# A fused encoder step: another order for the final norms, and larger last weight transfers

## The reference

```python
# per token: group by argmax, top 2 of the group's 8 experts, their weights in gate
hb = jax.nn.silu(xb @ w_gate[e]) * (xb @ w_up[e])     # (rows, 1024) @ (1024, 512)
y  = (hb @ w_down[e]) * gate                          # (rows, 512) @ (512, 1024)
x  = x + sum over the token's two experts of y
y_prompt, y_sample = rms_norm(x, final_norm_g)        # 512 rows, 64 rows
```

## Time and profile before

| | us |
|---|---|
| median of 3 runs | 1126.94 |
| lowest and highest run | 1126.05, 1127.9 |
| the profiled execution, its own time | 1129.78 |
| its span, from first to last instruction | 1128.04 |

### The profile page before, as it was taken

One profiled execution on the slowest core, in us unless ns is written; L12 is line 12 of the kernel. 1 busy time (PEld: TensorE's weight loads), 2 busy tenths in 40 slices (PEclk: granted clock), 3 DMA queues, 4 the chain that ended last, 5 costly groups with the idle time before them and its releaser, 6 DMA issues.

```text
span 1128.0 us, 11900 instructions
## 1 busy us (share of the span) xinstructions
PE 1045.7 (93%) x4726; PEld 542.4 (48%) x4726; DVE 461.2 (41%) x782; ACT 188.0 (17%) x489; POOL 98.9 (9%) x152
## 2 busy tenths in 40 slices
PE   8999999999999999999999999998886899977895
PEld 4577744555555447776656433333332233333331
DVE  4158734663773033013226753333322233322326
ACT  0156133434133001122101010000000000000001
POOL 1200001112005000000000010010000000000002
PEclk9999999999999999999999999998998899999998
DMA  7621140232234343221085899999999999999996
GB/s 262 242 71 35 46 154 1 69 124 85 76 112 154 135 149 149 75 84 67 1 338 196 352 373 426 428 427 426 426 427 426 428 426 426 427 426 426 421 412 241
DMA packets 52312, 281.14 MB, mean 249 GB/s; under 512 B 8200, under 2 KB 10160, under 8 KB 38946
## 3 DMA queue, kind: packets, MB, share of 16 engines
q1 hardware_dynamic: 45474, 262.57, 58.0%
q0 software_dynamic: 4752, 8.86, 2.1%
q10 hardware_dynamic: 2032, 8.96, 1.9%
HBM read 272.30 MB, written 22.81 MB: 262 GB/s over the span
## 4 chain that ended last, share of the span: by engine, by line
PE 78%; DMA 11%; SPq 5%; DVE 3%; issue 2%; ACT 0%; DVEq 0%; POOL 0%; ACTq 0%; POOLq 0%
PE banks L530 25%; PE banks L953 15%; PE banks L512 14%; DMA arena<-in_exp_w_down_dram 8%; PE banks L941 7%; SPq L1213 4%; PE banks L534 3%; DMA arena<-expert_rows 2%; PE banks L797 2%; PE score_pair L771 2%; DMA arena<-in_w_in_dram 1%; PE score_pair L596 1%; PE score_pair L900 1%; PE banks L630 1%; PE banks L499 1%
## 5 line engine op out<-in xcount | busy, mean ns | idle before, releaser
L530 PE MATMUL banks<-arena 128*128 128x512 f32 x640 | 283.9, 597 | 3.1 <-DMA arena<-in_w_in_dram 1.3
L953 PE MATMUL banks<-arena 128*64 128x512 f32 x1024 | 238.7, 623 | 34.8 <-issue 32.9
L530 PEld LDWEIGHTS banks<-arena 128*128 128x128 f32 x640 | 118.4, 190 | 144.4 <-issue 138.5
L953 PEld LDWEIGHTS banks<-arena 128*64 128x64 f32 x1024 | 82.1, 143 | 186.9 <-issue 185.6
L512 PE MATMUL banks<-arena 128*128 128x288 f32 x640 | 156.1, 406 | 0.0
L512 PEld LDWEIGHTS banks<-arena 128*128 128x128 f32 x640 | 121.4, 190 | 33.8 <-issue 0.4
L941 PE MATMUL banks<-arena 128*64 128x512 f32 x480 | 109.8, 611 | 19.2 <-DMA arena<-in_exp_w_down_dram 12.2
L1426 ACT ACTIVATE arena<-banks 128x512 f32<-128x512 f32 (+6 forms) x135 | 61.7, 493 | 388.9 <-PE banks L530 126.2
L1649 ACT ACTIVATE arena<-banks,arena 128x512 f32<-128x512 f32 x17 | 11.7, 687 | 405.8 <-PE banks L953 381.8
L941 PEld LDWEIGHTS banks<-arena 128*64 128x64 f32 x480 | 36.4, 140 | 82.2 <-issue 68.9
L2218 DVE SCALAR_TENSOR_TENSOR arena<-banks,arena 128x512 f32<-128x512 f32 x34 | 25.4, 750 | 99.6 <-PE banks L941 92.0
(11 more groups left out here) (333 smaller groups left out, 964.3 us busy)
## 6 DMA issues: line engine op xcount, KB each, us to landing
arena<-in_exp_w_gate_dram SPq DMA_DIRECT2D x28, 2048.0 KB, 32.9
arena<-in_exp_w_down_dram SPq DMA_DIRECT2D x28, 2048.0 KB, 33.5
arena<-in_exp_w_up_dram SPq DMA_DIRECT2D x27, 2048.0 KB, 35.2
arena<-in_w_in_dram SPq DMA_DIRECT2D x6, 2048.0 KB, 8.2
arena<-in_exp_w_down_dram SPq DMA_DIRECT2D x16, 512.0 KB, 11.0
arena<-in_exp_w_up_dram SPq DMA_DIRECT2D x6, 1024.0 KB, 8.2
expert_rows<-arena SPq DMA_DIRECT2D x4, 1152.0 KB, 7.8
out_dram<-arena SPq DMA_DIRECT2D x4, 1024.0 KB, 10.4
```

Source lines behind the costliest of these rows:

```text
L530: ins = mm(b[:, :], x, w[:, k, :], start=k == 0, stop=k == KC - 1)
L953: ins = mm(bank[own, :], xgT[:, k, own], w[j][:, k, :], start=k == 0, stop=k == KC - 1)
```

## The change

It has six parts, all in the last two passes and in what follows them.

1. Pass 15's gate matrices come as one transfer of 2 MB each, and its up matrices as two of 1 MB each. Down stays in four. PE waits once for the gate pieces, before its first step, and twice for up.
2. In pass 14, between gate and up, PE runs three matmuls into bank 5 whose result nobody reads.
3. The sample's two reads of `expert_rows` are issued first, then tiles 0, 1, 2, and tile 3 in two transfers, first all first rows and then all second rows (512 KB each).
4. On PE, after placing tiles 0, 1, 2, the sample follows at once, and tile 3 comes last.
5. DVE sums a tile's two read rows before it needs the placed rows (tiles 0 and 1). POOL does that sum for tile 2. For tile 3 DVE adds the placed rows to the first rows, then finishes tile 2, then adds the second rows. The order of the norms is 0, 1, sample, 2, 3.
6. ACT scales the sum of squares and adds epsilon (a second, one-column activation), and POOL only raises to the power.

```diff
-        late_ld = [[sem(f"last_{name}_quarter_loaded{k}") for k in range(4)] for name in ("gate", "up", "down")]
+        late_ld = [[sem(f"last_{name}_piece_loaded{k}") for k in range(n)] for name, n in (("gate", 1), ("up", 2), ("down", 4))]
...
-        FINAL_ORDER = (0, 1, 2, SAMPLE, 3)
+        FINAL_ORDER = (0, 1, SAMPLE, 2, 3)
...
-            def from_rows_by_quarters(bank, w, landed, signal):
+            def from_rows_by_pieces(bank, w, landed, signal):
...
-                    if k % 2 == 0:
-                        pe.wait_ge(landed[k // 2], 32)
+                    if k % (KC // len(landed)) == 0:
+                        pe.wait_ge(landed[k * len(landed) // KC], 32)
...
                     from_rows(SP_, i, banks[0], w[0:2], SP_.g_full, (1, 3, 5) if i == 0 else ())
+                    if i == PAIRS - 2:
+                        for _ in range(3):
+                            mm(banks[5], ident, ident.unsqueeze(1).broadcast_to([P, 4, P]), start=True, stop=True)
...
-            for t in range(SAMPLE):
-                if t == 3:
-                    pe.wait_ge(part_added, 1)
+            for t in range(3):
...
             ins.then_inc(f_full, 1)
+            pe.wait_ge(fsum, 1)
+            for half in range(2):
+                ins = place_last(3, half, True, True)
+            ins.then_inc(f_full, 1)
...
-            def load_quarters(which, e, over):
+            def load_pieces(which, e, over):
...
-                kq = 1 if which == 2 else 2
-                for k in range(4):
+                pieces = len(late_ld[which])
+                kq = (4 if which == 2 else KC) // pieces
+                for k in range(pieces):
...
+            t0, rows = TILES[SAMPLE]
+            for k in range(2):
+                sp.dma_start(yg_both[DEC * k:DEC * (k + 1), :], y_pairs[t0:t0 + rows, k, :]).then_inc(yg_ld[SAMPLE], 16)
+            for t in range(3):
+                t0, rows = TILES[t]
+                sp.dma_start(yg_rows[t], y_pairs[t0:t0 + rows].rearrange("t k n -> t (k n)")).then_inc(yg_ld[t], 16)
+            t0, rows = TILES[3]
+            sp.dma_start(yg[3][0], y_pairs[t0:t0 + rows, 0, :]).then_inc(yg_ld[3], 16)
+            sp.dma_start(yg[3][1], y_pairs[t0:t0 + rows, 1, :]).then_inc(last_row_ld, 16)
...
+            po.wait_ge(yg_ld[2], 16)
+            g.tensor_tensor(yg[2][0], yg[2][0], yg[2][1], ALU.add).then_inc(count_ready, 1)
             for done, t in enumerate(FINAL_ORDER):
                 rows = TILES[t][1]
                 po.wait_ge(fssq, done + 1)
-                inv_std(rstd[0:rows, 17 + t:18 + t], ssq[0:rows, 17 + t:18 + t], D).then_inc(frstd, 1)
+                g.tensor_tensor(rstd[0:rows, 17 + t:18 + t], ssq[0:rows, 17 + t:18 + t], neghalf[0:rows, :], ALU.pow).then_inc(frstd, 1)
...
+                act.wait_ge(sq_done, done + 1)
+                f(total_sq, total_sq, ACT.Copy, bias=EPS, scale=1.0 / D).then_inc(fssq, 1)
...
-            for t in range(3):
-                add_rows(t)
+            sum_rows(0, 1)
+            add_placed(0)
+            sum_rows(1, 2)
+            add_placed(1)
             ve.wait_ge(gf_ready, 1)
             finish(0)
-            add_rows(3)
-            for t in (1, 2, SAMPLE, 3):
-                finish(t)
+            finish(1)
+            ve.wait_ge(count_ready, 2)
+            add_placed(2)
+            finish(SAMPLE)
+            ve.wait_ge(yg_ld[3], 16)
+            ve.wait_ge(f_full, 5)
+            tt(halves(yg[3][0]), halves(yg[3][0]), placed[3], ALU.add).then_inc(part_added, 1)
+            finish(2)
+            ve.wait_ge(part_added, 3)
+            ve.wait_ge(last_row_ld, 16)
+            tt(yg[3][0], yg[3][0], yg[3][1], ALU.add).then_inc(fsum, 1)
+            finish(3)
```

More of the change, by code:

```diff
@@ L425, in encoder @@
         over_done = sem("over_passes_done")
-        y_zero, count_ready, hot_last_ready = sem("y_rows_zeroed"), sem("token_count_ready"), sem("last_one_hot_ready")
-        f_full, part_added = sem("last_rows_placed"), sem("first_row_added")
+        y_zero, count_ready, hot_last_ready = sem("y_rows_zeroed"), sem("token_count_then_row_sum_ready"), sem("last_one_hot_ready")
+        f_full, part_added = sem("last_rows_placed"), sem("two_rows_summed")
         gf_ld, gf_full, gf_ready = sem("final_gain_loaded"), sem("final_gain_spread"), sem("final_gain_copied")
@@ L430, in encoder @@
         yg_ld = [sem(f"y_rows_loaded{t}") for t in range(NT)]
-        fsum, fssq, frstd, fin_ready = (sem(f"final_{n}") for n in ("sum", "ssq", "rstd", "ready"))
+        last_row_ld = sem("second_y_rows_of_last_tile_loaded")
+        fsum, sq_done, fssq, frstd, fin_ready = (sem(f"final_{n}") for n in ("sum", "squares_summed", "ssq", "rstd", "ready"))
         fin_st = sem("final_stored")
         placed = [all_banks[:, 0:2, :], all_banks[:, 3:5, :], all_banks[:, 2:6:3, :], all_banks[:, 0:2, :], pair[0:DEC, :, :]]
-        FINAL_ORDER = (0, 1, 2, SAMPLE, 3)
+        FINAL_ORDER = (0, 1, SAMPLE, 2, 3)
         A = PsumRing(banks[0:3], a_full, a_free)
@@ L1004, in _ @@
                 if i == PAIRS - 1:
-                    from_rows_by_quarters(banks[0], w[0:2], late_ld[0], SP_.g_full)
+                    from_rows_by_pieces(banks[0], w[0:2], late_ld[0], SP_.g_full)
                     pe.wait_ge(gf_ld, 16)
@@ L1009, in _ @@
                     ins.then_inc(gf_full, 1)
-                    from_rows_by_quarters(banks[1], w[2:4], late_ld[1], SP_.u_full)
+                    from_rows_by_pieces(banks[1], w[2:4], late_ld[1], SP_.u_full)
                 else:
@@ L1247, in _ @@
                             sp.dma_start(gfin[0:1, :], a["final_norm_g"].rearrange("(o n) -> o n", o=1)).then_inc(gf_ld, 16)
-                        load_quarters(which, e, over)
+                        load_pieces(which, e, over)
             sp.wait_ge(y_st[0], 16 * (PAIRS // 2))
@@ L1683, in _ @@
                     over_loop(act, over_pair)
-            for t in FINAL_ORDER:
+            for done, t in enumerate(FINAL_ORDER):
                 rows = TILES[t][1]
@@ L1690, in _ @@
                 else:
-                    act.wait_ge(f_full, NT)
+                    act.wait_ge(f_full, 4)
                     total = placed[t]
-                f(scratch.rearrange("p (h n) -> p h n", h=2), total, ACT.Square, accum_out=ssq[0:rows, 17 + t:18 + t]).then_inc(fssq, 1)
+                total_sq = ssq[0:rows, 17 + t:18 + t]
+                f(scratch.rearrange("p (h n) -> p h n", h=2), total, ACT.Square, accum_out=total_sq).then_inc(sq_done, 1)
+                act.wait_ge(sq_done, done + 1)
+                f(total_sq, total_sq, ACT.Copy, bias=EPS, scale=1.0 / D).then_inc(fssq, 1)
         @block.vector
@@ L2296, in halves, with sum_rows, add_placed @@
                 return x.rearrange("p (h n) -> p h n", h=2)
-            def add_rows(t):
+            def sum_rows(t, n):
                 ve.wait_ge(yg_ld[t], 16)
+                tt(yg[t][0], yg[t][0], yg[t][1], ALU.add).then_inc(part_added, 1)
+                ve.wait_ge(part_added, n)
+            def add_placed(t):
                 ve.wait_ge(f_full, t + 1)
-                tt(halves(yg[t][0]), halves(yg[t][0]), placed[t], ALU.add).then_inc(part_added, 1)
-                ve.wait_ge(part_added, t + 1)
-                tt(yg[t][0], yg[t][0], yg[t][1], ALU.add).then_inc(fsum, 1)
+                tt(halves(yg[t][0]), halves(yg[t][0]), placed[t], ALU.add).then_inc(fsum, 1)
             def finish(t):
```

## The result

The changed kernel took 1132.51 us (median of 6 runs, 1131.42 to 1133.37); the kernel before, in runs beside it, 1127.89 (6 runs, 1126.05 to 1129.56). The ratio is 1.0042, interval 1.0030 to 1.0053: 4.6 us slower. I had said 2.45 slower, 1129.4, in 1127.3 to 1131.4. The direction is right, the size is not, and the time lies outside the range. Of the 3.1 us between 1129.4 and 1132.51, 0.95 is the base: I had added to 1126.94, and the kernel before took 1127.89 in these runs. The profiled execution, one of the six, took 1133.37 us. One run in this document, e5's of 1151.05 us, was in the kernel's slower state and is left out of its ratio.

A forecast was written before the change was run, and what follows sets the result against it. It took the weight stream to set the pace, then DVE and the sample's strand. Later tile 2 rows, POOL's sum and tile 3's bare norm moved the end from 1127.55 to 1130.0: 1126.94 + 2.45 = 1129.4, range 1127.3 to 1131.4.

The forecast's parts named there:

- the sample's mixing: Sample's reads ahead of the tiles: slowing of neighbouring transfers beyond their own 1.3 us, bounds 0 and 2.4, taken 1.5 us.
- the tail after tile 2: From the landing of tile 2's rows to the end of the last store: 18.0 us.
- the signs that I had named for a wrong forecast: POOL's sum starting by 1110 or taking 1.3 us, gate starting before 1079, or PE's clock half in gate.
- The wait of part 1: Pass 15's gate on PE waits for both whole matrices: starts 2.75 us later, DVE empties down 2.05 us late.
- the clock rival: PE's clock falls to half before pass 15's gate, costing 1.7 us on PE: 3.2 or 4 us slower; chance 0.30.
- POOL's sum: POOL's add of tile 2's two rows, ahead of its norm steps: 2.35 us, leaving DVE idle 2.7 before finish 0.
- Tile 3's bare norm: At the end, tile 3's norm with no other work to cover it: 2.15 us before its finish.
- Three matmuls: zero: The unread matmuls between gate and up of pass 14 take 2.6 us, absorbed by an idle gap and slack: zero.
- Part 6: nothing: Moving one short norm step from POOL to ACT: worth nothing, bounded by 0.5 us either way.
- The last store: Tile 3's store, now alone at the end: 2.7 us instead of 3.4 behind the sample's slow one.
- The rival that the mixing costs little: The sample's early reads slow neighbours by only 0 to 0.8 us: end 1.0 to 1.7 slower; chance 0.24.
- The faster one: The weight stream gains more than the rates say, 5 us, with 1.4 off the end: 1125.5 us; chance 0.08.

The follow-up runs named there:

- e5: Kernel before with only the sample's read made one 128-partition transfer, still last in the queue, and its sum matrix to match: 1126.21 us, ratio 0.9992.
- e1: Changed kernel with the sample's two 64-partition reads made one 128-partition transfer, and its sum matrix to match: 1131.82 us, ratio 1.0035.
- e4: Changed kernel with pass 15's last gate matrix in four pieces again: 1133.48 us, ratio 1.0055 of the kernel before.
- e8: Changed kernel with the sample's read as one 128-partition transfer and gate in four pieces, POOL's sum of tile 2 kept: 1128.36 us, ratio 1.0011.
- e6: Changed kernel with the sample's read as one 128-partition transfer and DVE summing tile 2, gate in one piece: 1131.87 us, ratio 1.0045 (4 runs).
- e12: The same kernel as e6, run again with more rounds: 1131.14 us, ratio 1.0031 (9 runs).
- e7: As e6 (one 128-partition sample read, DVE sums tile 2), but gate in four pieces again: 1126.87 us, ratio 1.0001.
- e3: Changed kernel with DVE, not POOL, summing tile 2's two read rows, between finishes 0 and 1: 1131.89 us, ratio 1.0036.
- e15: Kernel before with part 1 alone, gate in one transfer for each matrix and up in two: 1128.85 us, ratio 1.0013.
- e11: e9 without the three matmuls in pass 14: 1128.33 us, ratio 1.0006.
- e14: Kernel before with only the three matmuls in pass 14 added: 1127.83 us, ratio 1.0000.
- e9: e7 with DVE's order changed so that the finishes of the sample and tile 2 run during tile 3's norm: 1126.16 us, ratio 0.9990.
- e2: Kernel before with only the sample's two reads issued ahead of the four tiles: 1129.93 us, ratio 1.0020.

## Why the prediction was wrong

**The failed step is a size in part 3: the sample's mixing, "bounds 0 and 2.4, taken 1.5".** The mixing is what the sample's two half-partition transfers cost those in flight beside them, beyond their own length. It measured 4.9 us: 34.51 - 30.70 = 3.8 on down's last weights, and 44.31 - 34.51 = 9.8 from there to tile 2, of which 1.3 + 7.45 are lengths, another 1.05. e1 takes exactly this away (44.31 to 39.42), and e4 against e8 shows 5.0 us of time where nothing else hides it. The whole of the profile's miss of 2.7 us is here: 4.9 - 1.5 = 3.4, less 0.6 because the tail after tile 2 took 17.4 and not 18.0.

The bound was wrong because I read it from before's landings of tiles 2 and 3. There the sample's transfers were the last in the queue, and only the ends of the two tiles still in flight could suffer. Right behind down's weights they slowed all that was in flight with them: 2.39 MB moved in the 10 us at 239 GB/s, which at e1's 414 would have taken 5.8, 4.2 us less, with the DMA engines full in both. The cause is the half-partition form, 64 each, and not short rows or the stride: tile 3's two transfers of 128 partitions have the same 4 KB rows, 8 KB apart, and their packets, 87 of those in the stretch at 413 GB/s of after (1106 to 1110), took 0.16 us each. Reading `expert_rows` beside the weights is not the cause either: e1's single transfer does that, with the same bytes, at 414.

The rule that I weighed, the Trainium skill, page "SBUF — State Buffer", section "Door 1: The DMA port swizzle", has half of the ports out of reach of partitions 0 to 63. The trace agrees with the direction (the 128-partition form cures it), but its price for the sample's own bytes, 1.3 us by my estimate, is a quarter of what was lost in all. None of the signs that I had named for a wrong forecast came up; none of them was about this term.

**A second size was hidden behind it: the strand from the late gate.** The sum without the mixing gives 2.45 - 1.5 = 0.95 us slower. e1 measures that case: ratio 1.0035, 3.9 us, a time (1131.82) above my range by itself. So the right mixing alone would not have saved the forecast. The wait of part 1 was sized rightly: gate started at 1079.21, right on its landing, after 2.59 idle; the landings of gate, 9.79 against 9.80, and of down without the mixing, 30.7, are the forecast's; and in e6, with a full clock, down was emptied at 36.28 against 36.25. In after it does not count, since down waits for weights in any case (e4 gained nothing). It counts once the mixing is gone: 3.4 us from e12 to e7, where 2.05 was priced.

**The rest of that is, in part, the clock rival (0.30).** Behind the unfilled gap the granted clock was half in gate in four profiled executions (e1, e3, e12, e15) and full in two (after, e6). It cost 1.7 us each time. In those four, pass 14's gate had been at half clock too, and in the two it had not: an association in six executions, not a cause. Down fell as well, 1.7 more, in e1, e3 and e12, which I had not priced. But it also fell with gate on time (e8, e11, e14), so it can't all be put down to the late gate. In after's profile the clock did not fall, and if it had, POOL's sum would have covered it. In e3, with both falls, down was emptied at 39.69 and DVE's four adds were done by 44.64, and in after finish 0 starts at 47.37. e3, which has no sum on POOL, ended 0.8 us earlier than after. So the clock isn't the cause of the profile's miss.

**POOL's sum** was sized rightly, 2.35 us, with DVE idle 3.02 before finish 0 (forecast 2.7). With the mixing and the late gate gone it is worth about 1 us by the ratios and 1.5 by the medians (e8 less e7), with overlapping intervals. **Tile 3's bare norm** was 2.14 against 2.15; e9 covers it, and ends 1.4 us ahead of e7 in the profile. **Three matmuls: zero** holds (e14, 1.000). **Part 6: nothing** was not run alone; in after's profile the added one-column activation took 0.20. **The last store**, 2.7 forecast, took 2.6.

The rival that the mixing costs little (0.24) is refuted by e2 and by e4 against e8. The faster one (0.08) is too: the larger pieces brought gate 0.45 and down 0.7 forward, as the rates of the earlier trace rows said, and alone they lengthened the time if anything (e15). The prediction does not show how its 1.4 us came about: its rule of 18.0 us from tile 2's landing gives 2.5 for 5 us less of stream.

The loss of 4.6 us is thus of two strands of nearly the same length in the timed runs. One is the stream with the mixing; the other is PE from the late gate on, with its clock, and POOL's sum where the tiles meet it. Undoing one of them leaves the ratio at 1.0031 to 1.0055 (e1, e3, e4, e12), and only both removed bring it back (e8, 1.0011; e7, 1.0001).

**What stays open.** Why the clock fell behind 2.59 us of idle time in e15 and not behind 2.59 in e6, and how often it does so in pass 15 of the timed runs: they have only the mean granted clock of the whole execution. In e7 the three runs with the lowest mean (0.973 to 0.976) took 1130.1 to 1131.8 us and the other nine 1125.9 to 1128.9; in e12's nine runs time and mean clock show no relation. So how much of the 3.4 us of e12 against e7 is clock was not measured. The part that is only the wait was 1.2 in the profiles (down emptied at 36.28 in e6, 35.08 in e7).

## What to carry to other kernels

A cost read from a transfer's landing holds for the place where the transfer stood. Once it moves in the queue, it must be priced by what is in flight around it, so look at GB/s against the DMA share, and not at its own bytes. In this kernel it paid to let one transfer span all 128 partitions and to undo the new order of the rows in a matrix that was applied anyway. When a change has several parts and undoing any one gives nothing, undo them in pairs before calling a part harmless.

## What the runs showed of the hardware

- Two transfers of 256 KB to 64 partitions each, with 128-partition transfers in flight around them: 10 us at a DMA share of 1.03 and 239 GB/s (after). A 4 KB packet took 0.29 us there, against 0.16 outside. The same bytes to 128 partitions: 414 GB/s (e1), 4 KB packets at 0.16.
- An add of 128x1024 f32 with both operands in SBUF took 2.35 us on POOL and 1.23 on DVE (after); begun together, DVE's took 3.30 (e1). In e8 POOL's took 2.87, begun 0.57 us after a DVE add of the same kind:

```profile
1107.68 2.87 POOL L1408 TENSOR_TENSOR arena<-arena 128x1024 f32<-128x1024 f32 x1 [28.63 <-DMA arena<-expert_rows]
```

- After idle gaps of 2.1 to 2.6 us on PE, the granted clock was half (the 1.2 GHz level) for part of the next run in some executions and full in others of the same kernel (e6, e12). Where it fell in pass 15, it made 7.09 us into 8.76 or 8.78. The same happened to down behind idle gaps of 0.78 us (e1, e3, e8, e11, e12, e14), and did not in others with that gap (e6, e7, e9).
